# Odd mixer: the convolution's half of the output projection between the attention steps of the third head group

## The reference

```
proj = h @ w_in
qc, kc, vc, dc = split_cols(proj, (DIL_GROUPS * DIL_WIDTH, DIL_GROUPS * DIL_WIDTH, DIL_WIDTH, 2 * CONV_WIDTH))
...
for g, (window, dilation) in enumerate(DIL_PAIRS):
    o, lse = dilated_window_attention(qg[g], kg[g], v, slopes, window, dilation)
...
c_out = jnp.sum(wts[..., None].astype(v.dtype) * jnp.stack(outs), axis=0)
...
d_out = jax.nn.silu(layer_norm(conv, conv_ln_g, conv_ln_b))
return jnp.concatenate([c_out, d_out], axis=-1) @ w_out
```

## Time and profile before

| | us |
|---|---|
| median of three runs | 1073.78 |
| lowest and highest | 1069.72, 1075.07 |
| the profiled execution, its own time | 1065.87 |
| its span | 1063.9 |
| TensorE busy in it | 935.1 (88%) |
| VectorE, ScalarE busy | 416.1 (39%), 171.2 (16%) |
| mean granted clock of TensorE | 0.926 of full |

### The profile page before, as it was taken

The page is one execution under the profiler, slowest core; times in us unless marked ns, Lnnn a source line. Parts: engine busy times, 40 slices in busy tenths (PEclk is TensorE's granted clock), DMA queues, the critical chain, the costliest instruction groups (busy, mean ns, idle before and its releaser), DMA issues.

```text
span 1063.9 us, 13148 instructions
## 1 busy us (share of the span) xinstructions
PE 935.1 (88%) x5454; PEld 609.6 (57%) x5454; DVE 416.1 (39%) x984; ACT 171.2 (16%) x416; POOL 13.0 (1%) x51
## 2 busy tenths in 40 slices
PE   2699789499999899896999989987769999999994
PEld 2385554475556455452868777764356555555551
DVE  4846575442131311311796754543251111111112
ACT  2121120221111011102101422340111111111101
POOL 1000000000000000000000000000000000000000
PEclk9999789689999999898999989957859999999998
DMA  9996644647999999999377331170209799999941
GB/s 353 387 382 238 226 158 158 237 184 295 408 405 409 404 408 408 405 399 378 120 263 286 130 118 54 70 313 1 79 13 407 306 409 408 409 408 409 409 164 41
DMA packets 96079, 294.13 MB, mean 276 GB/s; under 512 B 2448, under 2 KB 3088, under 8 KB 96016
## 3 DMA queue, kind: packets, MB, share of 16 engines
q1 hardware_dynamic: 95184, 289.89, 70.7%
q10 hardware_dynamic: 688, 2.82, 0.7%
q0 software_dynamic: 144, 0.52, 0.1%
HBM read 292.18 MB, written 1.05 MB: 276 GB/s over the span
## 4 chain that ended last, share of the span: by engine, by line
PE 50%; issue 26%; DVE 11%; DMA 6%; SPq 4%; ACT 3%; POOL 0%; DVEq 0%; POOLq 0%
PE bank L618 13%; PE bank L614 9%; PE bank L801 9%; DMA ring<-w_gu_dram 4%; DVE gb L1190 4%; SPq L406 4%; PE bank L816 3%; PE bank L792 3%; PE bank L647 2%; PE bank L669 2%; PE bank L830 2%; PE bank L546 2%; PE bank L566 1%; DMA ring<-ada_w_dram 1%; PE bank L554 1%
## 5 line engine op out<-in xcount | busy, mean ns | idle before, releaser
L801 PE MATMUL bank<-ring,scr 128*64 128x256 f32 x2176 | 253.7, 387 | 9.4 <-DMA ring<-w_gu_dram 9.4
L801 PEld LDWEIGHTS bank<-ring,scr 128*64 128x64 f32 x2176 | 155.0, 139 | 102.2 <-issue 20.8
L618 PE MATMUL bank<-hT,ring 128*128 128x256 f32 x640 | 145.7, 389 | 0.0
L618 PEld LDWEIGHTS bank<-hT,ring 128*128 128x128 f32 x640 | 124.2, 196 | 17.9 <-issue 0.5
L816 PE MATMUL bank<-ring,scr 128*64 128x512 f32 x544 | 122.6, 592 | 0.0
L1190 DVE SCALAR_TENSOR_TENSOR gb<-ring,small,gb 128x512 f32<-128x512 f32 x140 | 105.5, 754 | 5.0
L1640 DVE TENSOR_TENSOR scr<-bank,scr 128x256 f32<-128x256 f32 x34 | 14.4, 424 | 205.3 <-ACT scr L1130 205.3
L792 PEld LDWEIGHTS bank<-scr,xh 128*128 128x128 f32 x576 | 71.6, 203 | 24.5 <-issue 22.0
L792 PE MATMUL bank<-scr,xh 128*128 128x128 f32 x576 | 77.8, 292 | 2.3 <-DVE scr L1612 2.3
L816 PEld LDWEIGHTS bank<-ring,scr 128*64 128x64 f32 x544 | 38.9, 137 | 64.4 <-issue 59.8
L1112 ACT ACTIVATE scr<-bank 128x256 f32<-128x256 f32 (+1 forms) x52 | 23.4, 450 | 300.5 <-PE bank L809 237.7
(11 more groups left out here) (215 smaller groups left out, 684.3 us busy)
## 6 DMA issues: line engine op xcount, KB each, us to landing
ring<-w_gu_dram SPq DMA_DIRECT2D x64, 2048.0 KB, 21.6
ring<-w_down_dram SPq DMA_DIRECT2D x32, 2048.0 KB, 21.4
ring<-ada_w_dram SPq DMA_DIRECT2D x24, 2048.0 KB, 17.6
ring<-od_w_in_dram SPq DMA_DIRECT2D x9, 2048.0 KB, 14.2
ring<-ev_w_in_dram SPq DMA_DIRECT2D x5, 2048.0 KB, 17.4
ring<-ev_w_out_dram SPq DMA_DIRECT2D x2, 2048.0 KB, 9.7
ring<-od_w_out_dram SPq DMA_DIRECT2D x2, 2048.0 KB, 11.0
xs<-x_dram ACTq DMA_DIRECT2D x1, 1024.0 KB, 5.8
```

Source lines behind the costliest of these rows:

```text
L618: ins = pe.matmul(banks[h][:, m * 256:(m + 1) * 256], w[:, c, (2 * h + m) * P:(2 * h + m + 1) * P], x_part[:, c, :], start=(c == 0 and m = ...
L801: ins = pe.matmul(b[64 * m:64 * m + 64, 256 * u:256 * u + 256], h[:, c, :], w[:, c, 512 * u + 256 * m:512 * u + 256 * m + 256], start=(fir ...
```

## The change

The third head group gets two entries for its first two F places: `fill(1, 18)` behind S1, and `fill(1, 20)` behind A1. For these the halves of the contraction change places: in the odd layer's output projection the even fill multiplies chunks 4 to 7 (the convolution's half) and the odd one chunks 0 to 3. The accumulation so begins at chunk 4 and ends at chunk 3. Behind the attention, where four fills stood, fills 19 and 21 are left. The wait of fill 18 for `dout_ready` moves with it, and so do the waits of fills 18 and 20 for their panels and their banks.

```diff
@@ fill @@
-                if l == 1 and kind == "out" and name == 0 and f % 2 == 0:
+
+                conv_first = l == 1 and kind == "out"
+                if conv_first and name == 0 and f % 2 == 0:
                     pe.wait_ge(dout_ready, 4)
+                first, last = (4, 3) if conv_first else (0, KC - 1)
+                half = 1 - f % 2 if conv_first else f % 2
                 x_part, w = (mixT if kind == "out" else hT), panel(pl.slot)
                 if f % 2 == 0:
                     pe.wait_ge(panel_in[pl.slot], pl.landed)
-                for c in range(4 * (f % 2), 4 * (f % 2) + 4):
+                for c in range(4 * half, 4 * half + 4):
...
-                                            start=(c == 0), stop=(c == KC - 1), skip_group_check=True)
+                                            start=(c == first), stop=(c == last), skip_group_check=True)
@@ odd @@
-                attention(1, 2, [])
+                attention(1, 2, [[F(18)], [F(20)]])
...
                 pe.wait_ge(turn_free, turn.n)
-                for f in range(18, 22):
-                    fill(1, f)
+                fill(1, 19)
+                fill(1, 21)
                 gate_row2(1)
```

## The result

| | before | changed |
|---|---|---|
| median, us (executions) | 1071.75 (4) | 1056.97 (4) |
| lowest and highest | 1068.60, 1075.07 | 1056.13, 1062.83 |
| ratio, 95% interval | | 0.988 (0.9847 to 0.9913) |
| the profiled execution, its time and span | 1065.87, 1063.9 | 1056.13, 1054.2 |

The change made the kernel faster, by 1.2% of its time. I had forecast faster, by 0.8% (ratio 0.9923), and a time of 1065.5 us in a range from 1061.8 to 1072.3. The measured time lies 4.8 us under the low end of that range. The profiled execution of the changed kernel is the fastest of its four.

What follows compares the result with a forecast made beforehand. TensorE at 1.2 GHz was taken to bound the third head group. Removing 13.8 us behind the last vector operation, less 5.5 us of delay, saves 8.3; off the median 1073.78 that gives 1065.5 us, range 1061.8 to 1072.3.

Steps and rivals of the forecast that it cites:

- fill 18, start to T0: Third head group, fill ahead of the first transpose: 8.6 us, starting at half clock, 2.8 us hidden in a wait.
- T0 to fill 20: Third head group, first block of rounds, between the two inserted fills: 5.9 us at full clock, against 9.55 at 1.2 GHz.
- fill 20, start to T2: Third head group, second inserted fill: delays everything behind it by 6.96 us, or 8.65 if the clock has just fallen.
- T2 to the end of S5: Third head group, second block of rounds up to the last scores: 4.2 us at full clock, against 7.8 at half.
- Rival 1: Third head group: clock returns in fills, is lost in each block of rounds; 0.6 us slower; chance 0.23 with half case.
- rival 2: Third head group: the clock does not come back at all; a loss of 10.9 us, 1084.7; chance 0.04.
- rival 3: Expert stage: waits for transfers starting at a fixed time, so the gain is hidden; 1073.8 us; chance 0.04.
- so I take the saving off the median: Whole kernel: the 8.3 us saving, summed on the profiled execution, is subtracted from the median, 1073.78, giving 1065.5 us.
- The clock falls to 1.2 GHz at 694.0: TensorE behind the third group's opening scores: the fall remains with the change, costing fill 18 1.7 us more.
- rival 4: Third head group: no clock fall at 694 and none later; 11.1 us saved, 1062.7; chance 0.16.
- No fill stands in the last part, so I take 12.2.: Third head group, end of the last scores to the last vector operation: stays 12.2 us; 11.1 at full speed.
- Removed behind the last vector operation: 13.8 us.: Output projection block behind the third head group: half of its 64 recorded matmuls leave, 27.6 / 2 = 13.8 us.

Runs made afterwards that it cites:

- experiments 8 and 9: Against the kernel before: 8 puts fill 18 behind S1 and fill 20 behind A5, ratio 0.9843; 9 adds gate's rows behind each block of transposes, 0.9833.

## Why the prediction was right and where it failed

| step | predicted | changed, first trace | second and third |
|---|---|---|---|
| fill 18, start to T0 | 8.6 | 7.0 | 8.7 |
| T0 to fill 20 | 5.9 | 5.9 | 5.9 |
| fill 20, start to T2 | 6.96 | 6.9 | 6.9 |
| T2 to the end of S5 | 4.2 | 4.2 | 4.2 |
| end of S5 to the last vector operation | 12.2 | 11.6 | 11.1 |
| from the transposes to the end of the fills | 34.0 - 13.8 = 20.2 | 22.3 | 23.1 |
| S1 to the end of the fills | 66.5 - 8.3 = 58.2 | 57.9 | 59.9 |

**Right.** The mechanism and most of its terms: a fill behind S1 that keeps or restores the clock, rounds of 2.55 us behind it, the stream behind the router shifted and not shortened (from the gather to the end 273.5 us before, 272.1 and twice 273.2 changed). Rival 1 (the clock lost in every block of rounds) and rival 2 (never back) did not occur in any of the three traces, and rival 3 is out, since `order` was written 8.2 us earlier and the end came earlier with it. The rule of the Trainium skill, "TensorE: Matmul & The Clock Gate", on PE-mode transpose, would have given rival 1. In the trace of fill 18 alone, four rounds with their transposes held 2.4 GHz for 14 us. What no run isolates is whether the transposes or the other two thirds of a round did it.

**Where it failed: the step from the saving to the time, "so I take the saving off the median", and with it the range.** The measured median lies 8.5 us under mine. 4.2 of them are the median of three that I took the saving off, 1073.78, where three later comparisons have 1069.4 to 1069.8; 1.0 is that the four executions of the first result lie below the fifteen together (1056.97 and 1058.0); 3.3 are the saving itself, 11.6 by these larger numbers in place of 8.3. I had allowed 1 us for the scatter of the runs, but 23 executions of before in one comparison lie between 1064.33 and 1075.35. A good part of the scatter arises ahead of the change: in these traces S1 ends at 690.8 to 700.0 us, behind a program that is the same. In the latest ones, 699.9 and 700.0, the delay of 6 us against the first trace of before is there at S0 of the first head group (588.7 and 588.8 against 582.49 us). In the changed kernel's second and third that S0 still stands at 582.7 and 582.8, and 3.5 us are added in the first two groups. Taken off the profiled execution, 1065.87, the same saving would have given 1057.6, near the measured time; that would have been luck in part, since that execution lies 3.7 us under the usual median of before. Seen as a ratio, 0.9923 lies inside the intervals of the two later comparisons and 0.001 above that of the first.

**Terms that were mis-sized.** Three, and they pull two ways:
- *"The clock falls to 1.2 GHz at 694.0, after ... matmuls that the change leaves alone."* It holds in two of three traces. In the first, with fill 18 alone, and in experiments 8 and 9, fill 18 ran at full speed. What ran behind S1 decides too: nothing in before, which lost the clock in every trace, dense matmuls here, which lost it in some. Worth 1.7 us in those executions; I had it only in rival 4.
- *"No fill stands in the last part, so I take 12.2."* The clock fell in the last part only in A4 or later, and VectorE waited 0.5 us or not at all for A5: 11.6 and 11.1.
- *"Removed behind the last vector operation: 13.8 us."* The block was costed at full clock. It took 15.0 and 15.8 us, since the clock was low in front of it and came back inside. In the kernel before it was 28.5 in its two later traces, against the 27.6 that I started from. With their 35.9 as the base, the removal is worth 12.8 to 13.6 us.

Against the usual 68.3 of before, the change is worth 8.4 to 10.4 us in the stretch, 9.1 by the mean of three traces. The ratios of the two larger comparisons, 0.9905 of 1069.6, are 10.2 us, and the medians differ by 11.6. So 1 to 2.5 us lie outside the stretch. The traces show a part of them behind the fills: from there to the end it is 303.7, 305.7 and 305.7 us in the three traces of before, and 304.2, 303.7 and 303.7 in those of the changed kernel. From S1 to the end the change is worth 10.4 to 12.0 us against the 374.0 of the later traces of before. But before has the 303.7 once too, so this may be chance: six of the fifteen executions of the changed kernel lie between 1057.5 and 1059.1 with a mean clock of 0.919 to 0.923, and none of my three traces is of one of them. Whether the change also alters, by way of the clock, what happens behind it was not settled.

## What to carry to other kernels

Look for the place where weak work on TensorE is followed by a wait. In this kernel it counted less how much independent work could be hidden in the wait than that some dense work stood in it: with the clock down, two rounds took 9.55 us in place of 5.9, and it stayed down for 38 to 41 us in the three traces of before. One fill at the right place gave all of this change's gain; the second had to go to the other wait, behind A5, to give anything, and this version (1050.9 us against 1058.1 and 1069.7) beats both kernels. And take a saving off a ratio or a median of many executions: where the clock falls differently from one execution to the next, the median of three was 4 us off here.

## What the runs showed of the hardware

- Matmuls that compute nothing made the kernel faster: 12 recorded matmuls (5.3 us) in a wait of 2.8 us gave 0.9951 (0.9926 to 0.9976).
- The fall behind S1 came in every trace without dense matmuls there (ten of ten, of four programs), 0.3 to 0.8 us behind the end of S1, although TensorE had been busy up to it, with single-column sums and 64-row scores. With dense matmuls behind S1 it came in three of eight traces, and the clock was back before that run of dense matmuls had ended.
- The same program on the same data takes clusters of times: the kernel before took 1069.4 to 1069.9 five times in one comparison, with a mean clock of 0.908, and 1066.6 to 1067.4 four times in the next, with 0.913. Two traces of the changed kernel on different chips agree to 0.1 us from S1 to the end, and a third is 1.5 us shorter there.
